# Swapping the stationary and the moving operand in a four-FFN decoder trunk

## The reference

```python
for i in range(2):
    h = rmsnorm(x, ln_gains[i, 0])
    x = x + 0.5 * swiglu(h, w_gate[i, 0], w_up[i, 0], w_down[i, 0])
    h = rmsnorm(x, ln_gains[i, 1])
    x = x + (moba_attention(h, w_qkv, w_o) if i == 0 else pool_mixer(h, pool_w, pool_scale))
    h = rmsnorm(x, ln_gains[i, 2])
    x = x + 0.5 * swiglu(h, w_gate[i, 1], w_up[i, 1], w_down[i, 1])
return rmsnorm(x, final_gain)
```

## Time and profile before

| | |
|---|---|
| median of 3 runs | 916.85 us (916.48 to 918.16) |
| span of the profiled execution | 914.7 us |
| PE busy | 896.7 us, 7431 matmul instructions |
| DVE busy | 563.5 us |
| ACT busy | 413.3 us |
| DMA | 158.96 MB, mean 174 GB/s |

### The profile page before, as it was taken

The page is one execution under the profiler, slowest core; times in us unless marked ns, Lnnn a source line. Parts: engine busy times, 40 slices in busy tenths (PEclk is TensorE's granted clock), DMA queues, the critical chain, the costliest instruction groups (busy, mean ns, idle before and its releaser), DMA issues.

```text
span 914.7 us, 17376 instructions
## 1 busy us (share of the span) xinstructions
PE 896.7 (98%) x7431; PEld 887.6 (97%) x7431; DVE 563.5 (62%) x591; ACT 413.3 (45%) x439; POOL 30.4 (3%) x49
## 2 busy tenths in 40 slices
PE   6999999999999999999999999999999999999996
PEld 6999999999998899999999999999999999999996
DVE  6965545649877597455554985545646976456444
ACT  6653433345554565334332663433425664334323
POOL 1650000000000000000000000000000000000000
PEclk9999999999999999999999999999999999999998
DMA  7775555535534247645644476555552475645601
GB/s 264 233 241 183 177 190 182 172 106 184 185 139 140 92 147 268 218 153 181 207 160 138 141 244 215 183 184 183 175 192 93 131 247 179 218 151 179 220 9 47
DMA packets 119112, 158.96 MB, mean 174 GB/s; under 512 B 2528, under 2 KB 106016, under 8 KB 119072
## 3 DMA queue, kind: packets, MB, share of 16 engines
q1 hardware_dynamic: 118976, 158.34, 52.8%
q10 hardware_dynamic: 96, 0.03, 0.0%
HBM read 157.32 MB, written 1.05 MB: 173 GB/s over the span
## 4 chain that ended last, share of the span: by engine, by line
PE 95%; DVE 2%; ACT 1%; DMA 0%; issue 0%; ACTq 0%; DVEq 0%
PE psum L358 30%; PE psum L359 30%; PE psum L360 30%; PE psum L477 1%; PE psum L475 1%; PE psum L479 1%; PE psum L533 1%; PE psum L519 1%; PE psum L508 1%; DVE w_lo L797 1%; DMA gains_rows<-in_final_gain_dram 0%; ACT w_hi L643 0%; ACT scratch L779 0%; PE psum L368 0%; ACT soft L662 0%; PE psum L366 0%
## 5 line engine op out<-in xcount | busy, mean ns | idle before, releaser
L358 PE MATMUL psum<-xg_hi,w_hi 128*128 128x256 f32 x1536 | 436.9, 284 | 0.9 <-DVE w_lo L830 0.6
L359 PE MATMUL psum<-xg_lo,w_hi 128*128 128x256 f32 x1536 | 435.4, 283 | 0.0
L360 PE MATMUL psum<-xg_hi,w_lo 128*128 128x256 f32 x1536 | 435.3, 283 | 0.0
L797 DVE TENSOR_TENSOR w_lo<-raw,w_hi 128x2048 fp32r<-128x2048 f32 x148 | 338.6, 2289 | 28.4 <-ACT w_hi L643 28.3
L358 PEld LDWEIGHTS psum<-xg_hi,w_hi 128*128 128x128 f32 x1536 | 295.5, 192 | 3.4 <-issue 2.7
L359 PEld LDWEIGHTS psum<-xg_lo,w_hi 128*128 128x128 f32 x1536 | 295.6, 192 | 0.0
L360 PEld LDWEIGHTS psum<-xg_hi,w_lo 128*128 128x128 f32 x1536 | 295.5, 192 | 0.0
L643 ACT ACTIVATE w_hi<-raw 128x2048 fp32r<-128x2048 f32 x148 | 277.9, 1903 | 17.3 <-DMA raw<-in_ffn_w_down_dram 8.0
L359 PE MATMUL psum<-h_lo,w_hi 128*128 128x256 f32 x704 | 199.2, 283 | 0.0
L360 PE MATMUL psum<-h_hi,w_lo 128*128 128x256 f32 x704 | 198.9, 282 | 0.0
L358 PE MATMUL psum<-h_hi,w_hi 128*128 128x256 f32 x704 | 197.3, 280 | 0.0
(11 more groups left out here) (96 smaller groups left out, 493.0 us busy)
## 6 DMA issues: line engine op xcount, KB each, us to landing
raw<-in_ffn_w_up_dram SPq DMA_DIRECT2D x44, 1024.0 KB, 5.4
raw<-in_ffn_w_down_dram SPq DMA_DIRECT2D x44, 1024.0 KB, 4.9
raw<-in_ffn_w_gate_dram SPq DMA_DIRECT2D x43, 1024.0 KB, 5.4
raw<-in_attn_w_qkv_dram SPq DMA_DIRECT2D x12, 1024.0 KB, 5.1
raw<-in_attn_w_o_dram SPq DMA_DIRECT2D x4, 1024.0 KB, 4.8
band<-in_x_dram SPq DMA_DIRECT2D x2, 512.0 KB, 4.9
raw<-in_ffn_w_gate_dram SPq DMA_DIRECT2D x4, 256.0 KB, 6.5
raw<-in_pool_w_dram SPq DMA_DIRECT2D x1, 1024.0 KB, 5.6
```

The source lines that it names most:

```text
L358: nc.tensor.matmul(out, hi, rhi, start=start, stop=False, skip_group_check=True)
L359: nc.tensor.matmul(out, hi, rlo, start=False, stop=False, skip_group_check=True)
L360: return nc.tensor.matmul(out, lo, rhi, start=False, stop=stop, skip_group_check=True)
L797: nc.vector.tensor_tensor(w_lo[:, n % SPL, :], raw[:, n % RAW, :], w_hi[:, n % SPL, :].bitcast(f32), ALU.subtract).then_inc(lo_split, 1)
```

## The change

- **Operands.** In gate/up, down and output projection the activations (128 features by 128 tokens) are stationary and the weights move, 512 columns at a time. Gate and up of a group are neighbours in the ring (a table SLOT replaces n % 6) and stream together: 256 columns of gate and 256 of up into one bank, for each half of the tokens. Down gives 512 features of one token half. Q and K keep the old form.
- **Layout.** x has tokens on partitions, in four pieces p (token half p//2, feature half p%2). 1/rms is a scalar per partition, which ACT applies inside silu and DVE inside the product. The squares are ACT's accumulated sums; the matmuls with ones go. For q and k PE spreads 1/rms over partitions once (`rstd_over_tokens`).
- **Transposes.** h is transposed by four PE transposes per group, in the middle of the next gate/up. x is transposed by PE for each norm: pieces 0 and 1 inside the last down tile, after p=1 and p=2, pieces 2 and 3 inside the next product, after k=1 and k=4. ACT and DVE read the transposed values from PSUM when they split them.
- **Splits.** In each step ACT and DVE split three tiles in a row behind silu and h, and also in the last step of FFN0, FFN1 and FFN2. Tiles 2 to 4 of FFN1 are split behind the norm that begins it, of FFN3 one ahead of it and two behind.
- **Attention.** The order of the first tiles is v, q, k. **Pool.** The output is computed with tokens on partitions; DVE applies 1/rms and the scale, then splits one tile, then updates x. `band` is built while FFN1 runs.
- **End.** No transposes; DVE scales x by 1/rms and a broadcast gain and four transfers write it.
- **Start.** Gate and up tile 0 are loaded by interleaved quarters; the token halves of x likewise.

```diff
-            def passes(out, hi, lo, rhi, rlo, start, stop):
-                nc.tensor.matmul(out, hi, rhi, start=start, stop=False, skip_group_check=True)
-                nc.tensor.matmul(out, hi, rlo, start=False, stop=False, skip_group_check=True)
-                return nc.tensor.matmul(out, lo, rhi, start=False, stop=stop, skip_group_check=True)
+            def early_transposes(norm):
+                def after(p):
+                    if p in (1, 2):
+                        x_transposes(norm, p - 1)
+                return after
+
+            def row_product(n, src_hi, src_lo, first=False, final=False, after=None):
+                hi, lo = row_tile(w_hi, n), row_tile(w_lo, n)
+                for p in range(PIECES):
+                    t, half = p // 2, slice((p % 2) * HALF, (p % 2 + 1) * HALF)
+                    for m in range(GM):
+                        mm(bank(Y + p), src_hi[:, m, toks(t)], hi[:, m, half], start=(first and m == 0))
+                        mm(bank(Y + p), src_hi[:, m, toks(t)], lo[:, m, half])
+                        last = mm(bank(Y + p), src_lo[:, m, toks(t)], hi[:, m, half], stop=(final and m == GM - 1))
...
+                    if after is not None:
+                        after(p)
...
+                    for t in range(TT):
+                        acc = acc_bank(b + t)
+                        for k in range(DC):
...
+                            mm(acc, xg_hi[:, k, toks(t)], hi[:, k], start=(k == 0))
+                            mm(acc, xg_hi[:, k, toks(t)], lo[:, k])
+                            last = mm(acc, xg_lo[:, k, toks(t)], hi[:, k], stop=(k == DC - 1))
...
+                            if j == 0 and t == 0:
+                                late_transposes(norm, k)
+                        if t == 0 and between is not None:
+                            between()
...
+                def h_transposes(j, i=0):
+                    par = (g0 + j) % 2
+                    pe.wait_ge(h_done, TT * (g0 + j + 1) + 2 * TT * i)
+                    for m in range(GM):
+                        for t in range(TT):
+                            last = nc.tensor.transpose(acc_bank(2 * par)[:, m, toks(t)],
+                                                       h_tok[:, par, t, m * P:(m + 1) * P], ident[:, :])
+                    last.then_inc(hT_done, 1)
...
+                gate_up(GROUPS - 1, between=lambda: h_transposes(GROUPS - 2))
+                down(GROUPS - 2, after=lambda p: h_transposes(GROUPS - 1) if p == 1 else None)
+                down(GROUPS - 1, final=True, after=after)
...
+        def step_tiles(f, j):
+            n0 = FFN_BASE[f]
+            first, end = n0 + 3 * j + 5, n0 + 3 * j + 8
...
@@ DVE, one step of an FFN
+                    for t in range(TT):
+                        dve.wait_ge(silu_done, TT * (g0 + j) + t + 1 + 2 * TT * i)
+                        nc.vector.scalar_tensor_tensor(out=h_tok[:, par, t, :], in0=acc_bank(2 * par + t)[:, 1, :],
+                                                       scalar=rstd[:, t:t + 1], in1=s_sb[:, t, :],
+                                                       op0=ALU.mult, op1=ALU.mult).then_inc(h_done, 1)
                     if j < GROUPS - 1:
-                        split_lo(n + 1, i)
+                        for n in step_tiles(f, j):
+                            split_lo(n, i)
                     dve.wait_ge(h_hi_done, g0 + j + 1 + 2 * i)
...
+                    if j == GROUPS - 1:
+                        for n in step_tiles(f, j):
+                            split_lo(n)
...
+            def boundary(norm):
+                update_x(norm, 0)
+                update_x(norm, 1)
+                x_rest(norm, 0)
+                update_x(norm, 2)
+                x_rest(norm, 1)
+                update_x(norm, 3)
+                x_rest(norm, 2)
+                x_rest(norm, 3)
+                inverse_mean(PIECES * (norm + 1))
                 refine_rstd(norm)
...
+            split_lo(FFN1 + 1)
+            boundary(2)
+            for n in range(FFN1 + 2, FFN1 + 5):
+                split_lo(n)
+            ffn(1)
```

More of the change, by code:

```diff
@@ new lines, in ffn @@
+                first = 0
+                if n0 == FFN0:
+                    for e in range(2):
+                        j = e + 1
+                        load(2 + 3 * e, cols, g[:, :, j * GW:(j + 1) * GW])
+                        load(3 + 3 * e, cols, u[:, :, j * GW:(j + 1) * GW])
+                        load(4 + 3 * e, rows, dn[:, j - 1])
+                    first = 1
+                with nc.Fori(first, PAIRS, engines=[sp.engine], hint_back_edge=True) as i:
+                    for e in range(2):
+                        group(e, i)
@@ L362, in statistics @@
-            def statistics(norm):
-                pe.wait_ge(sq_sum_done, norm + 1)
-                if norm not in (4, 6):
-                    nc.tensor.matmul(psum[:, 4, 0:SEQ], ones[:, :], sq_sum[:, :], start=True, stop=True)
-                for t in range(TT):
-                    last = nc.tensor.matmul(psum[:, 4, SEQ + t:SEQ + t + 1], sq_sum[:, t * P:(t + 1) * P],
-                                            ones[:, 0:1], start=True, stop=True)
-                last.then_inc(stats_done, 1)
@@ L425, in down @@
                     pe.wait_ge(h_lo_done, g0 + j + 1 + 2 * i)
[L426 to L430 removed]
+                    row_product(n, h_hi[:, par], h_lo[:, par], first, final, after)
+                gate_up(0)
+                gate_up(1, between=lambda: h_transposes(0))
                 down(0, first=True)
[L432 removed]
+                gate_up(2, between=lambda: h_transposes(1))
@@ L755, in _ @@
                                      ACT.Copy).then_inc(o_hi_done, 1)
-            boundary(2, FFN1)
-            ffn(FFN1, 1)
-            boundary(3, FFN2)
-            ffn(FFN2, 2)
-            round_x(4)
-            split_hi(FFN3 + 1)
-            root(4, rstd_p)
-            act.wait_ge(rstd_done, 5)
-            act.wait_ge(tile_used, used(POOL0))
-            for g in range(NPG):
-                for t in range(TT):
-                    last = nc.scalar.activation(pool_u[:, g, t, :], psum[:, g, t * GW:(t + 1) * GW], ACT.Copy,
-                                                scale=rstd_p[:, t:t + 1])
-                last.then_inc(pool_u_scaled, 1)
@@ L771, in _ @@
-            boundary(5, FFN3)
-            ffn(FFN3, 3)
-            for d in range(DC):
-                act.wait_ge(x_done, 6 * DB + d // 2 + 1)
-                if d % 2 == 0:
-                    square_x(d // 2)
-                nc.scalar.activation(xn[:, d, :], x[:, d, :], ACT.Copy, scale=gain(6, d)).then_inc(xn_done, 1)
-            root(6, rstd_p)
-            act.wait_ge(out_T, 1)
-            act.wait_ge(rstd_done, 7)
+            split_hi(FFN1 + 1)
+            boundary(2)
+            for n in range(FFN1 + 2, FFN1 + 5):
+                split_hi(n)
@@ new lines, in _ @@
+            boundary(2)
+            for n in range(FFN1 + 2, FFN1 + 5):
+                split_lo(n)
+            ffn(1)
+            boundary(3)
+            ffn(2)
+            boundary(4)
+            dve.wait_ge(scale_loaded, 16)
+            for p in range(PIECES):
+                t, c = p // 2, p % 2
+                if t == 0:
+                    dve.wait_ge(pool_u_half, 1)
+                else:
+                    dve.wait_ge(tile_used, POOL0 + 1)
+                nc.vector.scalar_tensor_tensor(out=pool_u[:, t, c * HALF:(c + 1) * HALF], in0=bank(p),
+                                               scalar=rstd[:, t:t + 1], in1=by_feature[:, c * HALF:(c + 1) * HALF],
+                                               op0=ALU.mult, op1=ALU.mult).then_inc(pool_u_scaled, 1)
```

849 lines of the change are left out of this document (426 added, 423 removed).

## The result

The changed kernel takes 946.38 us (median of 4 runs, 944.36 to 946.42); the kernel before took 917.5 beside it (4 runs). Ratio 1.0309, interval 1.0294 to 1.0323: 3.1% slower. Forecast were 893 and faster; the range ended at 914. The forecast's sum can be laid beside the profiled execution: 942.6 us where it said 887.6, the 3.5 us for the clock not yet in it. So 55 us have to be found. The profiled execution is the fastest of the four: the other three took 2 us more, at a mean granted clock of 0.982 to 0.984 instead of 0.986.

What follows compares the result with a forecast made beforehand. PE was taken as the bound, its 256-column matmuls by the weight load. Stream -80.0 us, h transposes +19.4, plus x transposes, waits, start, pool: 887.6 span, 889.8 median, plus 3.5 for clock: 893 us; range 874 to 914.

Steps and rivals of the forecast that it cites:

- reading a: 256-column float32r matmuls: the weight load takes about as long as the stream and bounds; 512 columns then step at 215.5 ns.
- All three say (a): Half-clock start, one-column loads and an fp32 matmul all show the weight load as the bound on the 120.0 ns pitch.
- By (b) the pitch would be 226: Kernel start at 1.2 GHz: a 13 ns cost per weight change would give 226 ns; 213.5 was read, bare stream.
- three loads of 113 ns: Statistics' one-column matmuls: three weight loads in 0.34 us, 113 ns each with no stream beside them.
- 1.7 ns over the stream for fp32: 256-column fp32 matmul ahead of the statistics: two instructions of 215 ns each, 1.7 above the bare 213.3.
- The pitch rival: Wide stream pays per weight change, 226.7 ns: 37 us more, 930 us; signs: pitch over 220, step above 16.3 us; 0.07 including 970 us case.
- readings (b) and (c): Matmul pitch: each weight change costs 13 ns (930 us), or float32r streams at 0.469 ns a column (970 us); together 0.07.
- a bit under two: Clock falls at long PE waits: four or five places could fall, about 2.2 us each, 0 to 10 us; 3.5 taken.
- Boundary waits: Ends of FFN0, FFN1, FFN2: PE waits for DVE's splits and update of x, 4.9 us three times, 14.7; absent: 875, chance 0.1.
- FFN1's start: Tiles 2 to 4 split only after norm 2: waits of 3.0 us for tile 3 and 1.4 for h_lo, sum +4.4.
- pool: Pool phase: late norm 4, pool_u, split and update of x make PE wait; 16.75 us instead of 12.0, +4.7.
- No wait: Steady FFN step: loads, splits and h arrive before PE wants them, so PE never waits; step of 15.97 us.

Runs made afterwards that it cites:

- experiment 1: PE alone, no reference: stretches of 48 matmuls in various widths and data types, plus transposes; 512-column float32r stepped at 226.7 ns, transposes at 109.1 ns.
- experiment 6: PE alone, no reference: 512-column matmuls beside DVE, ACT and PSUM traffic, narrow forms, one transpose ahead of 16; 226.7 ns with all traffic, 111.7 ns at 128 columns.
- the pad: 128 unused bytes ahead of h, added to the 913.04 us variant, so h and o lie at 128 modulo 2048; 906.45 us, ratio 0.987 to the kernel before.
- experiment 5: The changed kernel with each 512-column matmul issued as two of 256, new layout and order kept; 972.97 us, ratio 1.0604 to the kernel before.
- first kernel of experiment 3: The changed kernel with one split instead of three before the update of x at the ends of FFN0 and FFN1, two moved later; 934.19 us, ratio 1.0184.
- experiment 2: The changed kernel without three of the four transposes of h in each group (h wrong); 931.88 us, ratio 1.0166 to the kernel before.
- experiment 7: The changed kernel with splits at boundaries, starts and pool reordered and broadcasts issued by GpSimd; 913.04 us, ratio 0.9949 to the kernel before.

## Why the prediction was wrong

**The step that failed is the pitch.** The prediction took the 13.3 ns for the weight load (reading a), which a wide matmul would hide, and so put 215.5 ns where 226.7 were measured. "All three say (a)" was wrong; the pitch of the rival with 226.7 ns, and its sign, came true. 3,264 x 11.2 = **36.6 us** of the 55. Each of the three proofs had a hole:
-, "By (b) the pitch would be 226": they were taken at 1.2 GHz, where a 512-column matmul too takes 427 ns, bare stream. A cost that exists only at the full clock can't be excluded at half clock. And as the load takes 213 ns there (experiment 1), as long as the stream of 256 columns, the row could not tell a hidden load from one that bounds.
-, three loads of 113 ns: true (experiment 6: 111.7), but a load of 112 ns would make the pitch 112, not 120, and the 13.3 ns are there at 512 columns too, where the load has 213 ns of stream to hide under. Two numbers were close, and closeness was read as cause.
-, 1.7 ns over the stream for fp32: true for fp32 (experiment 1: 215.8 ns for an instruction of 256 columns in two passes), not for float32r. The value "of rows 5 as nearest" was one of another data type.

The pitch rival said that it "decides from a pitch of about 223 ns": 8 ns from the forecast's term turned the sign, and only 0.07 stood on readings (b) and (c) together.

**The rest of the 55 us.**
- Down and output projection 6.2 ns above gate/up, by where an operand lies: 1,152 x 6.2 = 7.1. Measured by the pad: 7.2.
- The swing behind the transposes: the step has 16.97 - 72 x 0.2267 - 24 x 0.0062 - 0.44 = 0.06 us more, 44 times 2.6. The transposes themselves were right at 110 ns (19.4 us).
- Clock: the granted clock fell to 0.50 at 27.92, 208.83, 345.36, 526.27 and 720.83 for 3.41 us each and at 737.89 for 6.83. PE worked in 21.9 us of them (the first busy time in each line below; 3.41 in the three falls not shown), and half of that, 10.9 us, is an estimate of what they cost. The sum of 887.6 had none of it, the forecast of 893 had 3.5, so this term was too small by 7.4. A fall of 3.41 us costs 1.7, where 2.2 was forecast; their number was the error. The forecast itself had five waits of 3 us or more and let "a bit under two" of them count.

```profile
27.92:31.33 3.41, 3.18 (x8) 2.51 (x9) 3.41 (x5) 2.88 (x4) 0.00 (x0) 0.50 0.99 314
...
345.36:348.77 3.41, 3.32 (x8) 2.64 (x9) 3.03 (x4) 1.18 (x3) 0.00 (x0) 0.50 1.06 359
...
737.89:744.72 6.83, 5.12 (x16) 4.29 (x17) 3.93 (x8) 1.67 (x5) 0.00 (x0) 0.50 0.54 169
```

- Boundary waits: forecast 4.9, measured 4.22 three times: -2.0. The mechanism and the place were right. The difference is the pitch again: PE comes to the wait behind 36 matmuls of down, 36 x 17.4 ns = 0.63 us later than forecast, while DVE keeps its time.
- Start: down 0 begins at 42.21, forecast 39.5; without the clock and the pitch, which are counted above, +0.5. FFN1's start has 3.8 us of waits instead of 4.4: -0.6. The tail is 1.1 shorter.
- Sum: 36.6 + 7.1 + 2.6 + 10.9 - 2.0 + 0.5 - 0.6 - 1.1 = 54.0. The last 1.0 fits pool, which took 20.8 us (725.51 to 746.30) instead of 16.75: 2.6 of the 4.0 are the clock, counted above, and 0.8 is a wait of 3.88 us for the update of x where 3.05 were forecast. Sums of this kind are good to about 1 us.

"No wait" in the steady step, the transposes and the direction of the boundary effects were right. Had only the pitch been 215.5, the rest would have left the span at 906 and the median near 908: within the range, and faster. So the pitch decided the sign; the clock alone would not have.

## What to carry to other kernels

A pitch must be measured in the same data type and at the same clock level as the one to be forecast; a row at half clock says nothing on a cost that a faster clock may expose. A wider instruction saves only the fixed part of its time, and two widths measured under the same conditions show how large that is (here 13.3 ns, paid once instead of twice). When the sign of a forecast hangs on one reading, put the neighbouring reading into the range. Place both operands of a 512-column float32r matmul alike modulo 256 bytes. Keep splits and DMA issues out from between the last product and the update that PE waits for. Look for waits of PE of about 4 us: each of the three here cost another 1.7 us by the clock.

## What was not expected of the hardware

- float32r matmuls of N = 256 to 512 columns at 2.4 GHz take N/2.4 + 13.3 ns, bf16 of 512 pays 2.5; why float32r pays more stays open.
- A 512-column float32r matmul is 2 to 7 ns slower when its operands start at different places modulo 256 bytes. With the place of the moving operand first: about 229 at (64,0) and (192,128), 232.3 with 128 between them, 233.3 at (0,64), (64,128) and (128,192). After a change the pitch swings for up to ten matmuls before it settles. The mechanism stays open. Down at 256 columns (experiment 5), with the same unlike places, stepped at 118.6 ns, no slower than gate/up's 119.9: the effect is shown for 512 columns alone.
- The clock does not follow the length of a wait alone. In the changed kernel, behind the first product, every wait of PE of 2.84 us or more had a fall to half clock in it or within 0.7 us behind it. But in the first kernel of experiment 3 the wait of 2.84 us at the start of FFN1 left the clock at 1.00, and in experiment 2 one of 3.85 us in pool did; in experiment 5 it fell after 2.53 us. Falls lasted 3.41 or 6.83 us. In experiment 1 it fell with no wait at all, 5.1 us into matmuls of 64 columns, and stayed at 0.50 for 17.07 us of matmuls of 64, 128 and 192 columns.
- ACT stood still for 4 us behind issuing one broadcast DMA: its next instruction began 2.8 us after PE had finished its input, and 0.03 us after it once GpSimd issued the DMA (experiment 7). On GpSimd it had no cost that can be seen.
- The best version, 906.45 us, is 1.3% faster than the kernel before; its steps save 44 x (17.28 - 16.81) = 20.7 us, and start, boundaries and pool still take back 9.5.
